# Rounded weight buffers with 32 words of room, and a starting word of its own for the weights of each product

## The reference

```python
def conv_ffn(x, w_up, conv_w, conv_b, w_down):
    h = causal_dwconv(x @ w_up, conv_w, conv_b)      # 2048 -> 11264
    gate, up = jnp.split(h, 2, axis=-1)
    return (jax.nn.gelu(gate) * up) @ w_down         # 5632 -> 2048

def first_block(...):
    for layer in range(DEPTH):                       # DEPTH = 2
        if layer % 2 == 0:
            z = x @ ev_w_in[j]
            ...                                      # recurrent mixers
            y = jnp.concatenate([y_a, y_b], axis=-1) @ ev_w_out[j]
        else:
            y = dsa_mix(x, od_w_in[j], ...) @ od_w_out[j]
        x = layer_norm(DN_ALPHA * x + y, ...)
        x = layer_norm(DN_ALPHA * x + conv_ffn(x, ...), ...)
        x = x + jax.nn.sigmoid(x @ ple_w_gate[layer]) * (p[layer] @ ple_w_proj[layer])
    return x
```

## Time and profile before

| What | Value |
|---|---|
| Median of three runs | 3287.43 us |
| Span of the profiled execution | 3284.6 us, so 2.8 us of the median lie around it |
| TensorE matmul, busy | 3232.2 us (98%), 21672 matmuls |
| TensorE weight load, busy | 2855.1 us (87%) |
| VectorE, busy | 2195.8 us (67%) |
| ScalarE, busy | 1667.5 us (51%) |
| GpSimd, busy | 24.5 us (1%) |
| Mean of the DMA traffic | 172 GB/s |

### The profile page before, as it was taken

One profiled execution on the slowest core, in us unless ns is written; L12 is line 12 of the kernel. 1 busy time (PEld: TensorE's weight loads), 2 busy tenths in 40 slices (PEclk: granted clock), 3 DMA queues, 4 the chain that ended last, 5 costly groups with the idle time before them and its releaser, 6 DMA issues.

```text
span 3284.6 us, 53186 instructions
## 1 busy us (share of the span) xinstructions
PE 3232.2 (98%) x21672; PEld 2855.1 (87%) x21672; DVE 2195.8 (67%) x2836; ACT 1667.5 (51%) x2138; POOL 24.5 (1%) x38
## 2 busy tenths in 40 slices
PE   9999999999999999999999999999999999999998
PEld 8888898888888888888888888888888888888887
DVE  6577767666676456676766666745675767647676
ACT  5574346555554335554555555533564456444563
POOL 0000000000000000011000000000000000000000
PEclk9999999999999999999999999999999999999999
DMA  7352145455444554534445445455544434444342
GB/s 279 143 210 67 57 167 200 181 188 196 179 185 175 184 190 183 190 119 180 164 181 199 182 186 198 159 186 192 188 168 185 171 129 167 186 175 167 129 171 112
DMA packets 47254, 563.64 MB, mean 172 GB/s; under 512 B 5072, under 2 KB 7264, under 8 KB 10720
## 3 DMA queue, kind: packets, MB, share of 16 engines
q1 hardware_dynamic: 47072, 561.06, 45.4%
HBM read 558.92 MB, written 2.12 MB: 171 GB/s over the span
## 4 chain that ended last, share of the span: by engine, by line
PE 90%; DVE 5%; ACT 3%; issue 2%; DMA 0%; SPq 0%; DVEq 0%; ACTq 0%
PE bank L863 40%; PE bank L849 21%; PE bank L968 10%; PE bank L973 5%; PE bank L1002 3%; ACT spl_r L1771 1%; PE bank L1468 1%; DVE ring L2506 1%; PE bank L784 1%; PE bank L788 1%; PE bank L782 1%; DVE spl_r L2506 1%; DVE xb L2506 1%; DVE xa L2506 0%; DVE scr L2506 0%
## 5 line engine op out<-in xcount | busy, mean ns | idle before, releaser
L2506 DVE TENSOR_TENSOR spl_r<-ring,spl_r 128x2048 fp32r<-128x2048 f32 (+2 forms) x429 | 961.3, 2242 | 485.8 <-ACT spl_r L1771 480.8
L863 PE MATMUL bank<-all_r,spl_r 128*128 128x512 f32 x4960 | 1196.6, 393 | 3.2 <-ACT spl_r L1771 3.2
L1771 ACT ACTIVATE spl_r<-ring 128x2048 fp32r<-128x2048 f32 x407 | 779.2, 1915 | 591.0 <-PE bank L849 484.1
L863 PEld LDWEIGHTS bank<-all_r,spl_r 128*128 128x128 f32 x4960 | 914.5, 188 | 189.5 <-issue 8.0
L849 PEld LDWEIGHTS bank<-all_r,spl_r 128*128 128x128 f32 x5008 | 642.1, 191 | 24.2
L849 PE MATMUL bank<-all_r,spl_r 128*128 128x256 f32 x5008 | 650.0, 283 | 0.0
L2506 DVE TENSOR_TENSOR dsp_r<-ring,dsp_r 128x1408 fp32r<-128x1408 f32 x126 | 204.8, 1625 | 206.4 <-ACT dsp_r L1771 206.2
L968 PE MATMUL bank<-scr_r,dsp_r 128*128 128x512 f32 x1386 | 338.8, 392 | 0.0
L1771 ACT ACTIVATE dsp_r<-ring 128x1408 fp32r<-128x1408 f32 x126 | 174.4, 1384 | 283.3 <-PE bank L973 283.1
L968 PEld LDWEIGHTS bank<-scr_r,dsp_r 128*128 128x128 f32 x1386 | 252.5, 189 | 47.4
L863 PE MATMUL bank<-scr_r,spl_r 128*128 128x512 f32 x1152 | 275.8, 391 | 2.9 <-ACT spl_r L1771 2.9
(11 more groups left out here) (437 smaller groups left out, 2673.9 us busy)
## 6 DMA issues: line engine op xcount, KB each, us to landing
ring<-in_up SPq DMA_DIRECT2D x88, 2048.0 KB, 7.8
ring<-in_down SPq DMA_DIRECT2D x64, 1408.0 KB, 6.0
ring<-in_ib SPq DMA_DIRECT2D x34, 2048.0 KB, 7.8
ring<-in_pg SPq DMA_DIRECT2D x16, 2048.0 KB, 7.8
ring<-in_out SPq DMA_DIRECT2D x16, 2048.0 KB, 7.9
ring<-in_in SPq DMA_DIRECT2D x12, 2048.0 KB, 7.7
ring<-in_ec SPq DMA_DIRECT2D x11, 2048.0 KB, 8.4
ring<-in_ea SPq DMA_DIRECT2D x8, 2048.0 KB, 10.5
```

The costliest lines, as they stand in the source:

```text
L863: mm(b[:, :], WHI[half][:, kk, :], pair(name, kk), start=kk == 0, stop=False, skip_group_check=True)
L1771: A(high[half], w[:, :, half * P:(half + 1) * P], ACT.Copy).then_inc(S["w_hi"], count)
L2506: return V.tensor_tensor(out, a, b, op)
```

## The change

The two constants that place the rounded buffers get room, and the views of the rounded weights are made anew for each product:

- The step from one buffer to the next goes from 2048 to `HALF` = 2080 words, and for `down` from 1408 to 1424 words. `scr` grows by 128 words; what shares the space (`LG`, `BF`) moves along.
- `BEGIN` gives for a product the word at which its high and its low weights begin within their buffer. `up0` has (2, 2), `up1` (4, 4), `in20` and `ib0` (8, 5), `in21` and `ib1` (16, 7), `down0` (2, 1), `down1` (6, 6), `out21` (0, 3), and `eb`, `ec`, `od_in` and `out20` have (0, 1). `ea`, `ev_out`, `od_out`, the queries, `pg0` and `pg1` stay at (0, 0).
- `SHIFTS` moves the activation pairs of `pg0` by 2 words and those of `pg1` by 1.

The numbers of instructions, their sizes, their order and their waits are the same.

```diff
+HALF = 2048 + 32
-SCR = 2 * (HHW + FC * 2 * P) - 2 * T
+SCR = 2 * (HHW + FC * 2 * P) - 2 * T + 4 * 32
+SHIFTS = {"pg0": 2, "pg1": 1}
+
+BEGIN = {"up0": (2, 2), "up1": (4, 4), "in20": (8, 5), "ib0": (8, 5), "in21": (16, 7), "ib1": (16, 7), "down0": (2, 1), "down1": (6, 6),
+         "eb": (0, 1), "ec": (0, 1), "od_in": (0, 1), "out20": (0, 1), "out21": (0, 3)}
...
-        WHI, WLO = ([spl_r[:, 4096 * h + o:4096 * h + o + 2048].rearrange("p (k n) -> p k n", n=P)
-                     for h in range(2)] for o in (0, 2048))
-
-        DHI, DLO = ([dsp_r[:, FC * P * (2 * h + o):FC * P * (2 * h + o + 1)].rearrange("p (k n) -> p k n", n=P)
-                     for h in range(2)] for o in range(2))
+        def rounded_halves(name):
+
+            high, low = BEGIN.get(name, (0, 0))
+            if name[:4] == "down":
+                return tuple([dsp_r[:, (FC * P + 16) * (2 * h + o) + begin:(FC * P + 16) * (2 * h + o) + begin + FC * P]
+                              .rearrange("p (k n) -> p k n", n=P) for h in range(2)] for o, begin in ((0, high), (1, low)))
+            return tuple([spl_r[:, HALF * (2 * h + o) + begin:HALF * (2 * h + o) + begin + 2048]
+                          .rearrange("p (k n) -> p k n", n=P) for h in range(2)] for o, begin in ((0, high), (1, low)))
+
+        WHI, WLO = rounded_halves("ea")
...
-                return scrv[:, a:b + 1:b - a, :]
+                shift = SHIFTS.get(name, 0)
+                shifted = scr_r[:, shift:shift + 80 * T].rearrange("p (a t) -> p a t", t=T)
+                return shifted[:, a:b + 1:b - a, :]
...
             def wide_half(name, k, half, i, first=False, count=1):
...
+                whi, wlo = rounded_halves(name)
...
-                        mm(b[:, :], WHI[half][:, kk, :], pair(name, kk), start=kk == 0, stop=False,
+                        mm(b[:, :], whi[half][:, kk, :], pair(name, kk), start=kk == 0, stop=False,
```

More of the change, by code:

```diff
@@ L415, in build @@
         AR = xb[:, :].rearrange("p (a t x n) -> p a t x n", a=8, t=2, x=2)
-        BF = [scr[:, SPL + 4096 * t:SPL + 4096 * t + 2048].rearrange("p (u x) -> p u x", u=16) for t in range(2)]
+        BF = [scr[:, SPL + 2 * HALF * t:SPL + 2 * HALF * t + 2048].rearrange("p (u x) -> p u x", u=16) for t in range(2)]
         GVB = [xtra[:, 1024 * t:1024 * (t + 1)].rearrange("p (u x) -> p u x", u=16) for t in range(2)]
@@ L538, in first_weights @@
             if name not in FIRST_SECOND_HALF or not half:
-                return WHI[half], WLO[half]
+                high, low = rounded_halves(name)
+                return high[half], low[half]
             return [all_r[:, 2 * X + o:2 * X + o + 2048].rearrange("p (k n) -> p k n", n=P)
@@ L549, in halves_of @@
         def halves_of(name):
-            return (DHI, DLO, FC) if name[:4] == "down" else (WHI, WLO, DT)
+            return (*rounded_halves(name), FC if name[:4] == "down" else DT)
         def rtiles(tensor, at_):
@@ L568, in build @@
         RHS.update({"ev_out": (YT, rtiles(scr_r, 4864), rtiles(scr_r, 0)),
-                    "pg0": (xav, rtiles(scr_r, 5632), rtiles(scr_r, 9728)),
+                    "pg0": (xav, rtiles(scr_r, 5632 + SHIFTS.get("pg0", 0)), rtiles(scr_r, 9728 + SHIFTS.get("pg0", 0))),
                     "od_out": (QQ, rtiles(scr_r, 6144), rtiles(scr_r, 10240)),
-                    "pg1": (xbv, rtiles(scr_r, 5632), rtiles(scr_r, 9728))})
+                    "pg1": (xbv, rtiles(scr_r, 5632 + SHIFTS.get("pg1", 0)), rtiles(scr_r, 9728 + SHIFTS.get("pg1", 0)))})
         for l in range(2):
@@ L706, in _ @@
             sp.wait_ge(S["g_done"], STEP0["ev_out"] - 2)
-            sp.dma_start(scr[:, SPL + 4096:SPL + 6144], dram["lg"][0]).then_inc(S["in_lg"], 16)
+            sp.dma_start(scr[:, SPL + 2 * HALF:SPL + 2 * HALF + 2048], dram["lg"][0]).then_inc(S["in_lg"], 16)
             sp.wait_ge(S["elem"], 3)
@@ L835, in from_high @@
                             pe.wait_ge(S["r_hi"], 4 * R_SPLIT.index(name) + kk // 4 + 1)
-                        mm(main, WHI[half][:, kk, :], rhi[:, kk, :], start=kk == 0, stop=False,
+                        mm(main, whi[half][:, kk, :], rhi[:, kk, :], start=kk == 0, stop=False,
                            skip_group_check=True)
@@ L842, in from_low @@
                             pe.wait_ge(S["r_lo"], 4 * R_SPLIT.index(name) + kk // 4 + 1)
-                        last_ = mm(low, WHI[half][:, kk, :], rlo[:, kk, :], start=False, stop=False,
+                        last_ = mm(low, whi[half][:, kk, :], rlo[:, kk, :], start=False, stop=False,
                                    skip_group_check=True)
@@ L848, in from_low_weights @@
                     for kk in range(first_, last):
-                        last_ = mm(main, WLO[half][:, kk, :], rhi[:, kk, :], start=False, stop=kk == DT - 1,
+                        last_ = mm(main, wlo[half][:, kk, :], rhi[:, kk, :], start=False, stop=kk == DT - 1,
                                    skip_group_check=True)
@@ L948, in down @@
                 l = int(name[4])
+                dhi, dlo = rounded_halves(name)
                 def unit(k):
@@ L964, in unit @@
                                 last_half()
-                            high, low = DOWN_FIRST if k + piece + half == 0 else (DHI[half], DLO[half])
+                            high, low = DOWN_FIRST if k + piece + half == 0 else (dhi[half], dlo[half])
                             pe.wait_ge(S["w_hi"], ready)
```

8 lines of the change are left out of this document (4 added, 4 removed).

## The result

The kernel after takes 3304.92 us, the median of four runs that lie between 3302.74 and 3305.28 us. The kernel before, beside it, takes 3287.06 us. The ratio is 1.0052, with a 95% interval of 1.0036 to 1.0068: slower by 18 us, 0.5%. I had predicted 3287.4 us and given no change the largest chance. The time lies inside the range of 3228 to 3322 us, and it is the slower of the two rivals whose sign came true.

What follows compares the result with a forecast made beforehand. The prediction took TensorE's matmul intervals to bound the kernel. Zero for moved starts and for the writers left 3284.6 + 0 = 3284.6 us of span, 3287.4 us with the 2.8 us around it; range 3228 to 3322 us.

Steps and rivals of the forecast that it cites:

- What bounds the kernel: Whole kernel: TensorE's matmuls, busy 3232.2 of 3284.6 us (98%); other engines count only once they make TensorE wait.
- What a moved start costs on TensorE: zero: Matmuls with moved operands: intervals unchanged, 0 us taken, from a range of 133 us gained to 49 us lost.
- the likeliest case: Whole kernel: no effect on TensorE, 3287.4 us, own range 3281 to 3294 us, chance 0.45.
- The count of what moves: TensorE matmuls with moved operands: 6026 wide and 7034 narrow, 13,060 in all.
- The faster rival: TensorE: weight load and streaming read hinder each other, a shift frees them; 66 us gained, 3221 us, chance 0.30.
- The slower rival: TensorE, above all odd starts: a start off the boundary costs an extra read; 35 us lost, 3322 us, chance 0.25.
- The 232 ns per wide matmul: Start of wide runs: if wide matmuls stayed at this interval, 22 us lost, 49 us with the narrow ones.
- The steps on the cover: ScalarE and VectorE weight writers: slower writes stay hidden by TensorE, 3.6 and 5.0 us to spare; zero taken.
- The chances: Whole kernel: faster by over 0.2% 0.30, within 0.2% 0.45, slower 0.25.

Runs made afterwards that it cites:

- the one with the short streams: Kernel before, with wide matmuls of `up0` streaming 384 columns and those of `up1` 256, other tokens left out: 3191.64 us in a single execution.

## Why the prediction was wrong

*What bounds the kernel.* Right. TensorE set the time in every kernel but the one with the short streams, and changes of its intervals went through to the end nearly in full.

*What a moved start costs on TensorE: zero.* This is the step that failed: the moved starts cost 18 us, between a gain of 34 ns and a loss of 253 ns per half by product, and undoing four products brought 15 of them back. I took agreement between products whose operands lie at multiples of 128 and 256 words as the nearest row, and wrote myself that this "only speaks for addresses at coarse grain". It was no evidence for the fine ones: of the nearly fifty pairs of moved weights tried in products of 16 tiles with unmoved activations, only (0, 18) leaves a half within 1 ns of 5567, and all undisturbed halves together run from 5507 to 5820 ns. The trace had the better hint, the 13 to 15 ns that fp32r matmuls lose and that the plain ones don't. I had called it the only stock on which addresses could draw, and then gave it no weight in the likeliest case. A fixed loss on every matmul, whose cause isn't known, is no ground for the value zero. The reading of the loss itself holds: single intervals start at 233, 236, 228, 233 and 231 ns, 232 in the mean, and settle at 226.7.

*The count of what moves.* The prediction counted only the products with begins or shifts, 13,060 matmuls, and took the room for neutral. But the room moves every buffer, the low ones to 32 words past a multiple of 64. That the halves still take 5567 ns with it was luck.

*The faster rival.* Its premise is borne out, its sign isn't. The loss depends on where the weights lie against the activations: equal distances of 32 gave equal times, and 8 with 8 gave that of 0 with 0. For given words the settled loss of a wide matmul is fixed. That two reads get in each other's way is the likeliest reading of this, but no run shows it. A change of this kind can gain: the products with (0, 1) gained 34 ns per half in the very kernel after, and (0, 20) everywhere gained 0.6%. Its price of 66 us was far too high, since the best half found gains 60 ns of the 16 x 11.3 + 16 x 9.2 = 328 ns that lie between it and the level of plain f32, under a fifth. And it took distance as such to be good, while for the high weights distance 0 was already about the best.

*The slower rival.* Its sign is right, its place and cause aren't. It put the cost at odd starts. But (0, 1) was faster, and the even begins (4, 4) carried 7.6 us; the low begins of 5 and 9, odd, are among the good ones, and 8 and 16, even and at the start of any line of four words, are not. Only the odd activations of `pg1` were as it said, and they were the costliest of all, 253 ns per half; yet with the weights moved along, activations at 2 cost as much as at 1. Its price of 35 us was twice the 18 that came. The 232 ns per wide matmul, taken from the earlier trace rows as the upper end, wasn't one: `up1` had 3736/16 = 233.5 and `pg1` 3836/16 = 239.8. The whole stayed inside the range because the other products lay lower.

*The steps on the cover held.* The rounding on ScalarE takes 1915 ns, to the digit that of the earlier trace rows, with writes that begin at words 0, 2, 4, 8 and 16:

```profile
L1787 ACT ACTIVATE spl_r<-ring 128x2048 fp32r<-128x2048 f32 x407 | 779.2, 1915 | 606.4 <-PE bank L864 501.3
```

VectorE's mean is 2293 ns, 2292 before. The idle time of TensorE ahead of the wide matmuls didn't grow. The room costs nothing in sum, as its own run shows.

*The chances.* They hung on whether fine words matter at all, which I held at 0.55, and on the sign then, which I held about even. The first should have been much higher. The sign was not to be had from the trace: it depends on which words were picked, and the lists tried gave both, +0.5% in the kernel after and -0.6% with the best pair.

*Other traffic as the cause.* The writes of ScalarE and VectorE into the same memory could have been a rival. The trace speaks against it: in the wide run of `pg1` that starts at 2416.46 us in the kernel after, the intervals are 240 ns both until 2418.64 us, while ScalarE writes high weights, and after it, while VectorE writes low ones. In the narrow run behind it the intervals go on between 121 and 126 ns after 2420.96 us, when neither writes weights.

What stays open is the rule. Shown is that three starts go into it: the high weights against the activations decide most of the wide run (3.64 us at 0 and 30, 3.68 to 3.75 at most others), the low weights move the narrow run and the first intervals of the wide one, and activations at 1, 2, 4 or 12 words lengthen the wide run even where the distances are kept. Why 19 and 20 words differ by 120 ns per half, why 0 and 30 are good for the high weights and 32 isn't, and how far the pattern repeats, no run here tells.

## What to carry to other kernels

Where TensorE bounds a kernel of fp32r products, the starting words of weights and activations are a parameter of its own, worth between -1% and +4.5% of a half's time here, and it can't be read off from tiles that agree at coarse steps. Give every product its own start, read the length of its runs from the chain of one profiled execution, and so measure a dozen starts in one run; then use the best one everywhere, and time that. Here the best found was: activations and high weights on a multiple of 64 words, the low weights 52 words past one, which is 20 words into a buffer that begins 2080 words after the high one. Count the words from one place for all operands, and not from the start of each buffer, for a step between buffers moves the starts as well.

## What the runs showed of the hardware

- The interval of fp32r matmuls with 512 columns lies between 227 and 240 ns in the mean of a run (3.63 to 3.84 us for 16) at a granted clock of 1.00, by the starting words alone. One column per cycle would be 213.3 ns. Runs with the same three starts agree to 2 ns in different products and kernels.
- Undisturbed halves of 16 and 16 take whole multiples of 6.67 ns in the mean of the two buffers: 5507 ns is 826 cycles of 2.4 GHz for each of 16 pairs of a wide and a narrow matmul, 5567 is 835, 5820 is 873, where one column per cycle is 768. With begins at 0 and no room the settled loss is 32 cycles per matmul, for 256, 384 and 512 columns.
- The Trainium skill's page "SBUF — State Buffer", under "Who interferes with whom", says that TensorE never waits on anyone, with independent ports for the stream and the load. As for other engines the trace agrees: the wide intervals of `pg1` are 240 ns whether ScalarE or VectorE writes weights beside them. As for the two reads of TensorE itself it speaks against full independence: a half takes 5620 ns at 32 words of distance and 5567 at 0, whichever operand moved. These runs don't show which port or memory is at work.
- Weight loads of 128, 64 and 32 columns are shown with 191, 134 and 108 ns: 0.8 to 0.9 ns per column over a fixed part of some 80 ns. Shorter loads don't shorten a wide matmul (230 and 231 ns in the mean, 228 with the full load), but they do shorten a narrow one, from 119 to 114 ns.
- ScalarE and VectorE write fp32r words at odd and even starts alike, 1915 and 2293 ns for 2048 words.
